# First-stage rotation through SBUF transfers, values ahead of the last query block, and sums at stage ends split between three engines

## The reference

```python
def rmsnorm(x, g):
    y = x * lax.rsqrt(jnp.mean(x * x, axis=-1, keepdims=True) + EPS)
    return y * g

def apply_rot(x, cos, sin):            # on each half of a head of 64 (rows, columns)
    x1, x2 = x[..., :16], x[..., 16:]
    return jnp.concatenate([x1 * c - x2 * s, x2 * c + x1 * s], axis=-1)

def attention_mixer(h, w_qkv, q_g, k_g, w_o, rope):
    q, k, v = jnp.split(h @ w_qkv, [1024, 1280], axis=-1)   # 16 query heads, 4 key heads, 4 value heads
    q = axial_rope(rmsnorm(q, q_g), rope)                   # norm of each head of 64
    k = axial_rope(rmsnorm(k, k_g), rope)
    p = softmax(q @ k.T / 8)
    return (p @ v) @ w_o

# first block:  attention, MLP (relu squared, 4096 wide), gated linear attention, MLP, final norm
# second block: three attention branches with gates, w_out, gated convolution FFN (2816 wide)
x = x + g1 * rmsnorm(y, norm_g[1])     # y = w_out's product
h = rmsnorm(x, norm_g[2]) * (1 + sc2) + sh2
x = x + g2 * rmsnorm(y2, norm_g[3])    # y2 = the FFN's product; x is the result
```

## Time and profile before

| | us |
|---|---|
| median of three runs | 2118.13 |
| lowest and highest | 2115.27, 2118.8 |
| profiled execution, its own time | 2123.1 |
| its span | 2121.2 |
| PE busy | 2051.5 |
| DVE, ACT, POOL busy | 1120.1, 747.2, 548.6 |

### The profile page before, as it was taken

One profiled execution on the slowest core, in us unless ns is written; L12 is line 12 of the kernel. 1 busy time (PEld: TensorE's weight loads), 2 busy tenths in 40 slices (PEclk: granted clock), 3 DMA queues, 4 the chain that ended last, 5 costly groups with the idle time before them and its releaser, 6 DMA issues.

```text
span 2121.2 us, 23916 instructions
## 1 busy us (share of the span) xinstructions
PE 2051.5 (97%) x9436; PEld 1642.1 (77%) x9436; DVE 1120.1 (53%) x1134; ACT 747.2 (35%) x789; POOL 548.6 (26%) x480
## 2 busy tenths in 40 slices
PE   7999999999999998999999999999999979999996
PEld 5666778888877887778888877788988858888884
DVE  4688445545554445454554554684434464545445
ACT  5555432222224433332222224345552242222322
POOL 0000189992000000179991002333220000000000
PEclk9999999999998999999999998999999989999998
DMA  4300144442222221144432222132123212223221
...
DMA packets 30812, 197.81 MB, mean 93 GB/s; under 512 B 3312, under 2 KB 3440, under 8 KB 7952
## 3 DMA queue, kind: packets, MB, share of 16 engines
...
## 4 chain that ended last, share of the span: by engine, by line
PE 91%; DVE 4%; ACT 2%; issue 1%; POOL 1%; DMA 0%; POOLq 0%; ACTq 0%; DVEq 0%; SPq 0%
PE ps L254 25%; PE ps L256 25%; PE ps L255 25%; PE ps L580 3%; PE ps L344 2%; PE ps L567 1%; PE ps L1425 1%; PE ps L285 1%; PE ps L287 1%; PE ps L286 1%; PE ps L1229 1%; PE ps L970 1%; PE ps L556 1%; PE ps L557 1%; ACT w_hi L216 1%
## 5 line engine op out<-in xcount | busy, mean ns | idle before, releaser
L216 ACT ACTIVATE w_hi<-w_raw 128x2048 fp32r<-128x2048 f32 x144 | 275.7, 1914 | 707.6 <-PE ps L256 707.3
L224 DVE TENSOR_TENSOR w_lo<-w_raw,w_hi 128x2048 fp32r<-128x2048 f32 x140 | 324.8, 2320 | 218.1 <-ACT w_hi L216 216.5
L254 PE MATMUL ps<-h_hi,w_hi 128*128 128x512 f32 x944 | 381.3, 404 | 7.9 <-DVE h_lo L390 4.0
L255 PE MATMUL ps<-h_lo,w_hi 128*128 128x512 f32 x944 | 372.7, 395 | 0.0
L256 PE MATMUL ps<-h_hi,w_lo 128*128 128x512 f32 x944 | 372.4, 394 | 0.0
L354 POOL TENSOR_TENSOR sq<-sq 128x1024 f32<-128x1024 f32 x12 | 38.6, 3217 | 886.3 <-ACT sq L330 734.8
L1213 POOL TENSOR_SCALAR ada_t<-ada_w,prm 128x256 f32<-128x256 f32 x192 | 222.0, 1156 | 9.8 <-DMA ada_w<-in_ada 8.9
L254 PEld LDWEIGHTS ps<-h_hi,w_hi 128*128 128x128 f32 x944 | 180.8, 191 | 52.5 <-issue 16.1
L256 PEld LDWEIGHTS ps<-h_hi,w_lo 128*128 128x128 f32 x944 | 180.1, 191 | 39.0
L255 PEld LDWEIGHTS ps<-h_lo,w_hi 128*128 128x128 f32 x944 | 180.7, 191 | 37.3 <-issue 1.4
L836 DVE TENSOR_TENSOR x<-x,ps 128x1024 f32<-128x1024 f32 x128 | 155.7, 1216 | 93.3 <-PE ps L256 93.3
...
## 6 DMA issues: line engine op xcount, KB each, us to landing
...
b_k<-b_k POOLq DMA_DIRECT2D x4, 256.0 KB, 5.5
b_kl<-b_kl POOLq DMA_DIRECT2D x4, 256.0 KB, 6.5
...
a_kh<-a_kh POOLq DMA_DIRECT2D x2, 256.0 KB, 3.7
```

The source lines that it names most:

```text
L216: act.activation(w_hi[:, slot], w_raw[:, slot], ACT.Copy).then_inc(hi_done, 1)
L224: dve.tensor_tensor(w_lo[:, slot], w_raw[:, slot], w_hi[:, slot].bitcast(F32), ALU.subtract).then_inc(split_done, 1)
L254: pe.matmul(out, w[0], h[0], start=start, stop=False)
L255: pe.matmul(out, w[0], h[1], start=False, stop=False)
```

## The change

In the first stage the partner rows are no longer made by PE. The weights' columns of queries and keys are laid out anew on the host (`ROPE_ORDER`), so that in each group of 64 partitions the first 32 and the last 32 are partners, and the sign is in the sine's table. POOL copies `a_g` into `a_sw` with the groups of 32 exchanged, four transfers of 32 partitions by 1024 (`swap`). DVE works on whole 128x1024 tiles: `cosine`, `sine`, `rotated`, `rooted`, `low`, and its low parts of a block come after the next `w_lo`. `a_sq` has one buffer, `a_g`, `a_sw` and `a_rot` two. `aux` is the sum of squares alone, stands after the first two k-tiles of the next block, and waits for `a_raw` and `a_rs` (the root of the block before). The values' block is the fifth (`V_BLOCK` = 4) and the last query block the sixth; its evacuation, sum, root and rotation are put into steps of the attention (`LAST`), and the quarters of the next weight's low part move from DVE's steps 10 to 13 to 20 to 23.

At norms 2, 4 and 8 (`APART`) ACT squares the third pair into a buffer of its own, DVE adds it (`dve_fold`) ahead of its add of the fourth pair, the fourth pair's squares are signalled by halves, and PE takes each half as it comes. The preloads of the tables for norms 2, 4, 6 and 8 stand ahead of the squares; the next weight's `w_hi` stands ahead of the last pair's squares at norms 2 and 4, and behind the root at norm 6.

```diff
+        APART = (2, 4, 8)
+        n_half = sem("n_half")
+        def third_square(n):
+            return (ff["f_r"][:, 1] if n == 8 else ml["m_r"][:, 0]).rearrange("p (a s) -> p a s", a=2)
         def act_square(act, n, j, src):
+            if n in APART and j >= 2:
+                if j == 3:
+                    act.wait_ge(n_fold, 2 * FOLDED.index(n) + 1)
+                to = third_square(n) if j == 2 else two(sq[:, 1])
+                for i in range(2):
+                    scale = G_ROOT[:, 2 * j + i:2 * j + i + 1] if n == 4 else 1.0
+                    ins = act.activation(to[:, i, :], src[:, 2 * j + i, :], ACT.Square, scale=scale)
+                    if j == 3 and i == 0:
+                        ins.then_inc(n_half, 1)
+                ins.then_inc(n_sq, 1)
+                return
...
-            else:
+            elif not (n in APART and j == 3):
...
+                if n in APART and j == 3:
+                    pe.wait_ge(*((n_half, APART.index(n) + 1) if i == 0 else (n_sq, 4 * n + 4)))
...
-            for j in (1, 2):
+            for j in (1,) if n in APART else (1, 2):
...
+        def dve_fold(dve, n):
+            dve.wait_ge(n_sq, 4 * n + 3)
+            dve.wait_ge(n_fold, 2 * FOLDED.index(n) + 1)
+            dve.tensor_tensor(two(sq[:, 0]), two(sq[:, 0]), third_square(n), ALU.add).then_inc(n_fold, 1)
...
-                if j == 3:
+                if j == 3 and i < 2:
...
-        V_BLOCK = N_QKV - 1
-        two = lambda ap: ap.rearrange("p (a s) -> p a s", a=2)
+        V_BLOCK, LAST = 4, 4
+        BLOCK_OF = (0, 1, 2, 3, 5)
...
-            def aux(j):
-                a = j
+            def aux(a):
                 if a == 0:
                     pe.wait_ge(con_in, 16)
                 pe.wait_ge(a_raw, a + 1)
                 if a >= 1:
-                    pe.wait_ge(a_rows, a)
+                    pe.wait_ge(a_rs, a)
                 for i in range(2):
-                    pe.matmul(ps[:, 4 + i, :], mat(HALVES), at_["a_sq"][:, a % 2, i * S:(i + 1) * S], start=True, stop=True)
-                for i in range(2):
-                    last = pe.matmul(ps[:, 6 + i, :], mat(ROT_A), at_["a_g"][:, a % 2, i * S:(i + 1) * S], start=True, stop=True)
+                    last = pe.matmul(ps[:, (0 if a == LAST else 4) + i, :], mat(HALVES), at_["a_sq"][:, i * S:(i + 1) * S], start=True, stop=True)
                 last.then_inc(a_aux, 1)
...
-                    pe_token_block(pe, b, b % 2, (j + 1) % 2, after=lambda t: aux(j - 1) if t == 1 else None)
+                    pe_token_block(pe, b, b % 2, (j + 1) % 2, after=lambda t: aux(j - 1) if t == 0 else None)
+                elif j == 0 or j > V_BLOCK:
+                    pe_block(pe, b, b % 2, HH, (j + 1) % 2, rows=0 if j == 0 else None)
                 else:
-                    pe_block(pe, b, b % 2, HH, (j + 1) % 2, rows=0 if j == 0 else None)
-                    if j >= 1:
-                        aux(j - 1)
+                    pe_block(pe, b, b % 2, HH, (j + 1) % 2, tiles=range(2))
+                    aux(j - 1)
+                    pe_block(pe, b, b % 2, HH, (j + 1) % 2, tiles=range(2, KT))
...
-                    pe.wait_ge(a_rs, V_BLOCK)
-                    pe.wait_ge(a_rows, V_BLOCK)
+                    pe.wait_ge(a_rs, LAST)
                     pe.wait_ge(a_dup, 64)
                     pe.wait_ge(a_ready, 2)
                 if u == 4 * TT:
-                    pe.wait_ge(a_ready, V_BLOCK)
+                    pe.wait_ge(a_ready, LAST)
+                if u == 12 * TT:
+                    pe.wait_ge(a_ready, LAST + 1)
...
+                if s == 2:
+                    aux(LAST)
...
+            def evacuate(a):
+                j = BLOCK_OF[a]
+                act.wait_ge(block_done, B_QKV + j + 1)
+                if a >= 1:
+                    act.wait_ge(a_aux, a)
+                if a >= 2:
+                    act.wait_ge(a_rows, a - 1)
+                act.activation(two(at_["a_sq"][:]), a_pair(j), ACT.Square)
+                act.activation(two(at_["a_g"][:, a % 2]), a_pair(j), ACT.Copy, scale=pc("kg" if a == 0 else "qg")).then_inc(a_raw, 1)
...
             for j in range(V_BLOCK):
...
+                evacuate(j)
+                next_hi(act, B_QKV + j + 2, (B_QKV + j) % 2)
                 if j >= 1:
-                    root(j - 1)
                     q_hi(j - 1)
-            root(V_BLOCK - 1)
-            q_hi(V_BLOCK - 1)
+                root(j)
+            take_v()
+            next_hi(act, B_QKV + V_BLOCK + 2, (B_QKV + V_BLOCK) % 2)
+            q_hi(LAST - 1)
...
+                if s == 0:
+                    evacuate(LAST)
                 if s == 4:
-                    take_v()
+                    root(LAST)
+                if s == 14:
+                    q_hi(LAST)
...
+            def cosine(a):
+                dve.wait_ge(a_raw, a + 1)
                 if a == 0:
                     dve.wait_ge(rope_in, 32)
-                if a >= 1:
-                    dve.wait_ge(a_qhi, 2 * a)
-                for i in range(2):
...
+                if a >= 2:
+                    dve.wait_ge(a_qhi, 2 * a - 2)
+                dve.tensor_tensor(two(at_["a_rot"][:, a % 2]), two(at_["a_g"][:, a % 2]), twice_row(at_["a_cos"][:]), ALU.mult)
+            def sine(a):
+                dve.wait_ge(a_swap[a % 2], 64 * (a // 2 + 1))
+                sw = two(at_["a_sw"][:, a % 2])
+                link(dve, dve.tensor_tensor(sw, sw, twice_row(at_["a_sin"][:]), ALU.mult))
+            def rotated(a):
+                rot = at_["a_rot"][:, a % 2]
+                link(dve, dve.tensor_tensor(rot, rot, at_["a_sw"][:, a % 2], ALU.add))
+            def rooted(a):
+                rot = at_["a_rot"][:, a % 2]
                 dve.wait_ge(a_rs, a + 1)
-                dve.scalar_tensor_tensor(out=at_["a_rot"][:], in0=at_["a_rot"][:], scalar=1.0 if j == 0 else HD ** -0.5,
+                dve.scalar_tensor_tensor(out=rot, in0=rot, scalar=1.0 if a == 0 else HD ** -0.5,
                                          in1=at_["a_rs"][:], op0=ALU.mult, op1=ALU.mult).then_inc(a_rows, 1)
...
+            def low(a, r):
...
+            for j in range(V_BLOCK + 1):
                 next_lo(dve, B_QKV + j + 2, (B_QKV + j) % 2)
                 if j >= 1:
-                    rope(j - 1)
-            rope(V_BLOCK - 1)
+                    for r in range(2):
+                        low(j - 1, r)
+                if j < V_BLOCK:
+                    cosine(j)
+                    sine(j)
+                    rotated(j)
+                    rooted(j)
...
+                if s == 6:
+                    cosine(LAST)
+                if s == 8:
+                    sine(LAST)
+                if s == 10:
+                    rotated(LAST)
+                if s == 12:
+                    rooted(LAST)
+                if s in (16, 18):
+                    low(LAST, s // 2 - 8)
+                if 20 <= s < 24:
+                    quarter_lo(dve, B_WO0 + 1, (B_WO0 + 1) % 2, s - 20)
...
+            def swap(a):
+                pool.wait_ge(a_raw, a + 1)
+                if a >= 2:
+                    pool.wait_ge(a_rows, a - 1)
+                for i in range(4):
+                    to, of = slice(32 * i, 32 * i + 32), slice(32 * (i ^ 1), 32 * (i ^ 1) + 32)
+                    pool.dma_start(at_["a_sw"][to, a % 2], at_["a_g"][of, a % 2]).then_inc(a_swap[a % 2], 16)
+            swap(0)
+            swap(1)
...
+            for a in range(2, LAST + 1):
+                swap(a)
...
+            act.preload_act_table_set("natural_log_exp_and_others")
             for q in range(4):
+                if q == 3:
+                    next_hi(act, b0 + 2 * u + 3, (b0 + 1) % 2)
                 act.wait_ge(m_add, 4 * (MLP_UNITS * i + u) + q + 1)
                 act_square(act, n, q, x)
-            next_hi(act, b0 + 2 * u + 3, (b0 + 1) % 2)
...
+                if q == 3:
+                    dve_fold(dve, 2 * i + 2)
                 mlp_dve_add(dve, i, u, q, b0 + 2 * u + 1)
...
+                if q == 3:
+                    dve_fold(dve, 8)
                 add(u, q, b0 + 3 * u + 2)
...
+        act.preload_act_table_set("natural_log_exp_and_others")
         e["act_proj"](act, 2, B_WOUT, 6, e["y"], 6)
-        act.preload_act_table_set("natural_log_exp_and_others")
         e["act_std"](act, 6, 6)
+        e["split_hi"](act, B_FFN + 1, (B_FFN + 1) % 2)
...
```

81 lines of the change are left out of this document (35 added, 46 removed).

## The result

The changed kernel takes 2089.01 us (median of 4 runs, 2088.29 to 2093.94) against 2117.15 us of the kernel before (4 runs, 2115.27 to 2118.8). The ratio is 0.9864, 95% interval 0.9848 to 0.9880: 28.1 us less, where 25.0 were forecast (2093.1). The profiled execution took 2088.29 us around a span of 2086.6, at a mean granted clock of 0.989 (before: 2121.2 at 0.981).

What follows compares the result with a forecast made beforehand. PE, busy 97% of the 2121.2 us span, was taken to bound the kernel. Terms summed to -25.0 us: 2123.1 to 2098.1, less 5.0 from profile to median, 2093.1; own range 2089 to 2097, the 8-in-10 range reaching to 2101.

Steps and rivals of the forecast that it cites:

- rotation off PE, stall, its clock, last sum moved: Projection blocks: rotation matmuls 8.56, idle wait 4.19, lowered clock 1.49 and moved sum 1.71 us saved; attention starts 15.95 us earlier.
- start of the attention, first to ninth score: Attention's first steps: new waits and root against less low clock; taken as 0 us, bounds -0.6 and +1.1.
- rotation in the attention: Attention, steps 6 to 23: DVE falls 3.3 us behind, 1.9 of it free; +1.4 us, bounds 0 and 3.3.
- first MLP's end: End of MLP 1: earlier sums and a clock that holds in two cases of three; -2.4 us, bounds -3.1 and 0.
- second MLP's end: End of MLP 2: earlier sums and a clock that holds in two cases of three; -4.1 us, bounds -4.9 and -1.7.
- w_out: End of the w_out projection: w_hi and table load moved, so the logarithm starts earlier; -1.1 us.
- FFN's end, sums: End of the FFN: last sums of squares end at 2103.4 against 2104.9; -1.6 us.
- FFN's end, table load: End of the FFN: one early table load serves logarithm and exponential, removing the load between them; -1.3 us.
- B: Projection blocks and attention: each swap issue waits for the DVE operation under way; +3 to +4 us, 2097; chance 0.12.
- C: MLP ends and attention's start run at half pace, the clock gives nothing back; 2097.6, or 2099.5 with DVE's full lag; chance 0.16.
- D: Projection blocks: swaps landing later than about 12 us make the chain set the period; slower than before, near 2125; chance 0.03.
- E: Projection blocks: clock or DMA traffic brings a new hole, worth half of the first stage; 2100; chance 0.07.

Runs made afterwards that it cites:

- e3: Changed kernel with the five pairs of rotation matmuls put back on PE beside the transfers, their result unused; 2099.65 us.
- e11: Changed kernel with every swap held back on GpSimd by 8 small memsets, 4.6 us, before its first issue; 2089.41 us.
- e4: Changed kernel with the last query block's sum at step 4 of PE instead of 2 and its root at step 6 of ScalarE instead of 4; 2091.70 us.
- e10: Changed kernel with the last block's high halves and w_lo quarters spread out in the attention, its sum at step 3 and its root at step 5; 2089.79 us.
- e8: Changed kernel with every swap held back on GpSimd by 18 small memsets, 10.4 us, before its first issue; 2099.29 us.

## Why the prediction was right, step by step

Shifts are those of PE's or ScalarE's landmarks between the two profiled kernels.

| step | forecast us | measured us |
|---|---|---|
| rotation off PE, stall, its clock, last sum moved | -15.95 | -15.97 (first score from first block, 90.66 to 74.69) |
| start of the attention, first to ninth score | 0 (-0.6 to +1.1) | 0.0 (10.90 to 10.88) |
| rotation in the attention | +1.4 (0 to 3.3) | +1.1 (scores 9 to 64, 96.80 to 97.91) |
| first MLP's end | -2.4 (-3.1 to 0) | -3.33 |
| second MLP's end | -4.1 (-4.9 to -1.7) | -4.86 |
| w_out | -1.1 | -1.04 |
| FFN's end, sums | -1.6 | -1.8 |
| FFN's end, table load | -1.3 | -1.3 |
| sum | -25.0 | -27.2 |

**Right, and for its reason:** the projection blocks. PE's side products were the price (e3), the transfers stayed under DVE's other work, and at 2.8 us a landing was nearer to free than the 4.7 I had bounded it by with a transfer twice as large. e11 shows that another 4.6 us would have been hidden too.

**Right in size, half wrong in its mechanism:** the cost of the rotation inside the attention, forecast at 1.4 us and measured at 1.1. I had DVE fall 3.3 us behind through all that it is given from step 6 to 23. The four passes cost nothing. The four w_lo quarters in a row, the last item of that sum, cost 0.59 us. The other 0.54 were ScalarE's two high halves ahead of an exponential, a step that I had dismissed ("has room for its two passes": it has the time, but in its order they stand ahead of what PE waits for). That the size came out is luck. Room by busy share isn't room in the queue.

**Right by two errors:** the attention's start. At the full clock I had worked out 10.3 us, and it took 10.88 at the full clock, where before 10.90 held some low clock. The fourth turn comes 9.57 us after the first score, not 9; e4 and e10 show that the root's place decides, and only the gap between the maxima is free.

**The terms that were mis-sized:** the clock. At both MLP ends I took the better clock for two cases of three; it came in full (the eight records in 3.62 and 3.71 us, where they had taken 5.24 and 6.50), so the ends gave their full -3.33 and -4.86. That is 1.7 us of the 4.1 by which the median undercut 2093.1. In the profiled pair the rest is in places for which I had no term: between landmarks the work behind the first MLP's end shrank by 1.6 us up to the second one's, that behind the second by 3.2 up to w_out, the norm ahead of the FFN by 0.9 and the FFN by 1.1. (The 4 to 5 us of each stretch in the table above hold the ends and the start themselves, so they are not to be added to these.) Part of that was only the profiled run before, which lay 5 us above its median; the changed kernel's lay 0.7 below its own, so that my shift of 5.0 from profile to median did not carry over. The input landed 0.7 us earlier, for no reason of the change's.

**The rivals.** B (issues wait for DVE) is refuted by the issues of e8, for operations on two SBUF inputs. C (the clock gives nothing back) was the reverse of what happened. Its price was also inconsistent with my own sums: at half pace the ends come to -8.0 + 4.4 = -3.6 us together, not -3.1. D begins somewhere between 4.6 and 10.4 us of further delay (e11, e8). E showed no hole in the blocks.

**Open.** Why the first MLP's end is granted 0.96 in some programs and 0.92 or 0.93 in others with the same rows there; I had no run that sets it. And why the clock behind the second MLP's end stays at 0.96 with a hole of 2.3 us and is 0.91 with one of 3.2, while at the FFN's end 2.85 did not lower it, was seen and not explained.
